# Another order of waits at four places of a two-block transformer kernel

## The chip, the core and the metric

The kernel runs on one core of a Trainium2 chip. A core has five engines with instruction queues of their own, which run in order and wait for each other by semaphores: TensorE (PE: matmuls and transposes, into PSUM), VectorE (DVE), ScalarE (ACT), GpSimd (POOL) and SyncE (SP, which issues the weight DMAs). PSUM has eight banks of 128 x 512 floats. The metric is the time of one execution on the device, in microseconds.

## What is computed

One sequence of 512 tokens of width 1024 goes through two blocks, all in float32. Cut to what matters here:

```
# first block
h = rmsnorm(x); proj = h @ w_in            # fox q,k,v; sb q,k,v; forget logits
x += concat(rmsnorm(fox_attention(...)), rmsnorm(stick_breaking_attention(...))) @ w_out
x += memory_cross_attention(rmsnorm(x), rmsnorm(mem)) @ w_mo
u = causal_dwconv(rmsnorm(x) @ w_up); gate, val = split(u)
x += (silu(gate) * val) @ w_down           # 2816 gated features
h = rmsnorm(x) * gain                      # the first block's output
# second block, layer 0: gated MLP with spatial gating
z = gelu(rmsnorm(h) @ a_w_in); u, v = split(z); v = layernorm(v)
sv = w_s (masked, per 128-token block and group) @ v + b_s
h += (u * sv) @ a_w_out                    # u, v are 2048 wide
h += relu(rmsnorm(h) @ w1)**2 @ w2
# layer 1: latent attention, then the same MLP; a last rmsnorm
```

## The kernel before

**Products.** A float32 product is made of three matmuls: each operand is a high half (rounded to float32r by ScalarE) and a low half (the rest, by VectorE), and `split_sum` (L424) adds hi x hi, lo x hi and hi x lo in one bank (L432 to L434, or L469 to L471 where tokens are stationary). Activations lie feature-major in `x` (eight tiles of 128 x 512); their halves are in `h_hi`/`h_lo` (eight tiles) and `g_hi`/`g_lo` (four).

**Weights** come as a stream of chunks of 1 MB (`weight_stream`, L61), two slots, each loaded by SP into `raw`, split by ScalarE (`split_high`, L1639, two pieces a chunk, line L1649) and then by VectorE (`split_low`, L935, L944). ScalarE waits until PE has used up the chunk two before (a count of finished tiles that the stream gives, `ENDS`); entries `("tiles", n)` of the stream stand for tiles that need no weights. Both engines call the splits at fixed places of their programs, written out by hand.

**Tiles.** PE fills four banks in turn. `next_bank` waits until the tile four before has been taken; `full` counts a finished tile; on VectorE `take` waits for the next full tile and empties it, always in order. So a VectorE queue that is busy with something else holds PE once four banks are full.

**Attention** is a pipeline over 32 units (head, block of 128 queries), one a step: at step s PE makes the scores of unit s, the values of unit s-3 and the transposes of unit s-2, and then runs what `n_after(s)` gives: other products in pieces, to fill the steps. Unit s-2 needs its probabilities: in fox attention from ScalarE, in sb (stick-breaking) attention from ScalarE's two sigmoids and VectorE's scan and product (L1051, L1054). Beside fox run the memory keys and the sb values; the last three steps (32 to 34) have nothing beside them. The sb queries and keys follow (`by_feature`), then sb attention. Beside it (`beside_sb`, PE L687, DVE L1216, ACT L1812) four transposes per tile turn the mixed, normed fox result into features (`turn_mixed`, L634; ScalarE's high half and VectorE's low half, `take_mixed`, L1191, empty them) at steps 0 and 1, memory values run at steps 2 to 25 in pieces of six matmuls, two pieces a step at first (`MEM_VALUES_AT`), and half of the output product at 26 to 33. `SB_PIECES` are the steps at which VectorE splits a piece of weights (ScalarE one step earlier). After each eight units VectorE copies the bank of results (L1169) and ScalarE sums squares of it.

**The gated feed-forward.** Pairs of 256 gated features (granules) go through `up`, a convolution and a gate, into `t_buf`; their halves go to two of the four `g` tiles. `down` (PE L506, DVE L1013, ACT L1695) multiplies two granules: its first half of four output tiles, then four more, each added to `x`. The eleventh granule (number 10) is left over and goes through `back(10)` (PE L486) after the last `down`. Its halves are made at the end of that `down` (`then=`), since the four `g` tiles are still being read. `back("final, mix0")` on VectorE and ScalarE also makes the next halves in `h` and the squares for two statistics (`two_stats`, L769; VectorE's sums L983).

**The gated MLP of block two.** Four groups of values `gm_v`, then sixteen feature tiles of `gm_u` (taken at L1030, gelu at L1890). After tile 13 PE makes group 0 of the spatial products (`spatial`, L794, four tiles), tiles 14 and 15, and `out_half(0, 0)`, which reads the halves of the gated product in `g`. On VectorE: `take_spatial` (L1396, with biases made just before, L1391), `times_u` (L1404), `low_of_gated` (L1409); on ScalarE `high_of_gated`.

## Time and profile before

| | us |
|---|---|
| three runs | 2068.95, 2066.1, 2068.57 |
| median | 2068.57 |
| the profiled execution | 2069.1 |
| its span in the trace | 2065.8 |
| PE busy in it | 2014.6 (98%) |
| DVE / ACT / POOL busy | 1155.7 / 757.4 / 203.9 |
| mean granted clock of PE | 0.993 |

A busy share says how long an engine had work in it, not how fast it ran: PE's clock has two levels, 2.4 and 1.2 GHz, and PEclk is the share of full speed that was granted. A timeline row gives the start, the duration, the engine, the source line, what is written from what, how many instructions were merged, and in brackets the idle time ahead of it with what ended it. Matmul durations overlap: one of 128 x 512 has 0.39 us, but the next starts 0.23 us later.

### The profile page before, as it was taken

To read this page: it belongs to the slowest core of one execution; us is meant where nothing else is said; L and a number is where in the kernel's file an instruction comes from. 1 tells how busy PE (TensorE), PEld (TensorE's weight loads), DVE (VectorE), ACT (ScalarE), POOL (GpSimd) and SP (SyncE) were. 2 spreads that over 40 slices of the span, in tenths; PEclk is the share of its full clock that TensorE was granted. 3 is DMA by queue.
4 is the path that set the end of the run, shared out by engine and by line. 5 is a ranking of instruction groups with operands and counts; after the bars stand their busy time and mean duration, and the time that the engine had idled before them with its cause. 6 is when DMAs were issued, how large, how long until landed. Compare 5 with 4: busy or idle time off the path is not lost. (4 is left out here: it accounts for less than half of the span.)

```text
span 2065.8 us, 23160 instructions
## 1 busy us (share of the span) xinstructions
PE 2014.6 (98%) x9535; PEld 1668.3 (81%) x9535; DVE 1155.7 (56%) x1585; ACT 757.4 (37%) x1201; POOL 203.9 (10%) x108
## 2 busy tenths in 40 slices
PE   7999999999999999999999999999999999999998
PEld 5897888788888888788878888888877788888887
DVE  6543576568756666846557643543487665333333
ACT  4354354235433333533223422233343443322224
POOL 1000000000000000000000222222221002122221
PEclk9999999999999999999999999999999999999999
DMA  5231212212233233233312233223223012232321
GB/s 167 83 99 45 82 62 72 92 42 86 98 102 100 85 102 102 82 106 98 102 62 82 88 102 102 85 99 102 82 66 102 21 62 84 100 102 91 95 101 61
DMA packets 141224, 180.51 MB, mean 87 GB/s; under 512 B 9664, under 2 KB 102976, under 8 KB 141120
## 3 DMA queue, kind: packets, MB, share of 16 engines
q1 hardware_dynamic: 139232, 177.52, 26.5%
q8 instruction: 75, 1.23, 0.2%
q10 hardware_dynamic: 1632, 1.51, 0.2%
q14 instruction: 29, 0.24, 0.0%
q0 software_dynamic: 256, 0.02, 0.0%
HBM read 176.91 MB, written 2.10 MB: 87 GB/s over the span
## 5 line engine op out<-in xcount | busy, mean ns | idle before, releaser
L432 PE MATMUL bank<-h_hi,w_hi 128*128 128x512 f32 x1376 | 542.4, 394 | 7.1 <-DVE arena L1556 4.5
L433 PE MATMUL bank<-h_lo,w_hi 128*128 128x512 f32 x1376 | 537.3, 391 | 0.0
L434 PE MATMUL bank<-h_hi,w_lo 128*128 128x512 f32 x1376 | 537.3, 390 | 0.0
L1649 ACT ACTIVATE w_hi<-raw 128x1024 fp32r<-128x1024 f32 (+2 forms) x336 | 332.7, 1033 | 512.4 <-PE bank L434 456.3
L432 PE MATMUL bank<-g_hi,w_hi 128*128 128x512 f32 (+1 forms) x988 | 384.1, 389 | 9.6 <-DVE g_lo L958 4.3
L434 PE MATMUL bank<-g_hi,w_lo 128*128 128x512 f32 (+1 forms) x988 | 378.8, 383 | 0.0
L433 PE MATMUL bank<-g_lo,w_hi 128*128 128x512 f32 (+1 forms) x988 | 378.7, 383 | 0.0
L402 POOL TENSOR_TENSOR w_lo<-raw,w_hi 128x1024 fp32r<-128x1024 f32 (+1 forms) x78 | 189.5, 2430 | 1658.9 <-ACT w_hi L1649 1658.9
L1002 DVE TENSOR_TENSOR resid<-bank,resid 128x512 f32<-128x512 f32 x288 | 195.9, 689 | 263.2 <-PE bank L434 262.8
L944 DVE TENSOR_TENSOR w_lo<-raw,w_hi 128x1024 fp32r<-128x1024 f32 (+1 forms) x258 | 304.8, 1206 | 67.7 <-ACT w_hi L1649 66.8
L432 PEld LDWEIGHTS bank<-h_hi,w_hi 128*128 128x128 f32 x1376 | 259.4, 189 | 64.5 <-issue 11.0
L433 PEld LDWEIGHTS bank<-h_lo,w_hi 128*128 128x128 f32 x1376 | 259.6, 189 | 55.2 <-issue 1.9
L434 PEld LDWEIGHTS bank<-h_hi,w_lo 128*128 128x128 f32 x1376 | 259.4, 189 | 54.1
L432 PEld LDWEIGHTS bank<-g_hi,w_hi 128*128 128x128 f32 x988 | 186.4, 189 | 48.9 <-issue 12.6
L434 PEld LDWEIGHTS bank<-g_hi,w_lo 128*128 128x128 f32 x988 | 186.2, 188 | 36.5
L433 PEld LDWEIGHTS bank<-g_lo,w_hi 128*128 128x128 f32 x988 | 186.4, 189 | 34.8
L596 PE MATMUL bank<-arena 128*128 128x128 f32 (+8 forms) x928 | 178.6, 328 | 3.3 <-ACT arena L1728 1.4
L596 PEld LDWEIGHTS bank<-arena 128*128 128x128 f32 (+1 forms) x928 | 133.3, 191 | 28.3 <-issue 9.6
L1496 DVE SCALAR_TENSOR_TENSOR arena<-bank,rstd 128x512 f32<-128x512 f32 x64 | 44.0, 691 | 177.4 <-PE bank L434 177.2
L1937 ACT ACTIVATE arena<-arena 128x512 f32<-128x512 f32 x64 | 40.5, 633 | 221.6 <-DVE arena L1496 221.6
L1728 ACT ACTIVATE arena<-bank 128x128 f32<-128x128 f32 (+3 forms) x112 | 48.2, 431 | 174.1 <-PE bank L588 174.1
L958 DVE TENSOR_TENSOR g_lo<-arena,g_hi 128x512 fp32r<-128x512 f32 x110 | 73.7, 688 | 30.7 <-ACT g_hi L1938 20.6
(199 smaller groups left out, 1686.8 us busy)
## 6 DMA issues: line engine op xcount, KB each, us to landing
raw<-w SPq DMA_DIRECT2D x64, 1024.0 KB, 5.2
raw<-w_up SPq DMA_DIRECT2D x22, 1024.0 KB, 5.1
raw<-a_w_in SPq DMA_DIRECT2D x16, 1024.0 KB, 5.2
raw<-w_in SPq DMA_DIRECT2D x12, 1024.0 KB, 5.4
raw<-w_down SPq DMA_DIRECT2D x11, 1024.0 KB, 4.9
raw<-w_mkv SPq DMA_DIRECT2D x8, 1024.0 KB, 5.5
raw<-a_w_out SPq DMA_DIRECT2D x8, 1024.0 KB, 5.0
raw<-w_out SPq DMA_DIRECT2D x4, 1024.0 KB, 5.0
```

The costliest lines, as they stand in the source:

```text
L402: G.tensor_tensor(lo, src, hi.bitcast(F32), ALU.subtract).then_inc(w_split_pool, 1)
L432: nc.tensor.matmul(dst, a_hi, b_hi, start=(k == 0), stop=False)
L433: nc.tensor.matmul(dst, a_hi, b_lo, start=False, stop=False)
L434: last = nc.tensor.matmul(dst, a_lo, b_hi, start=False, stop=(k == n - 1))
L596: ins = nc.tensor.matmul(dst, a, b, start=first, stop=last)
L944: V.tensor_tensor(lo, src, hi.bitcast(F32), ALU.subtract).then_inc(w_split, 1)
L958: V.tensor_tensor(lo, src, hi.bitcast(F32), ALU.subtract).then_inc(ready, 1)
L1002: take(lambda b: V.tensor_tensor(x[:, n, :], b[:], x[:, n, :], ALU.add))
L1496: take(lambda b: V.scalar_tensor_tensor(r_buf[:, j, :], b[:], 0.0, rstd[:, 0, :], ALU.max, ALU.mult))
L1649: A(hi, src, ACT.Copy).then_inc(w_hi_done, 1)
L1728: A(prob_t[:, u % 2, 0:nk], pt_bank[:, 0:nk], ACT.Copy).then_inc(pt_taken, 1)
L1937: A(t_buf[:, j, :], r_buf[:, j, :], ACT.Square)
```

## The change

Four places change; the arithmetic and the number of instructions stay.

1. **Gated MLP.** VectorE takes the four spatial tiles before it splits the chunk that it split after tile 13, and makes the gated low halves before it takes tiles 14 and 15. ScalarE makes the high halves before the gelus of tiles 14 and 15.
2. **Last granule.** The halves of granule 10 go to tiles 6 and 7 of `h`, which nothing reads then, and are made before the last `down`, not at its end. `back(3, in_h=True)` reads them (3 is the pair of h tiles). Because the next halves overwrite tiles 6 and 7, ScalarE waits in every such `back` for PE's eighth tile before it writes tile 6.
3. **Beside sb.** Memory values run at steps 0 to 23 (two pieces a step up to 7), the mixed fox tiles are turned at steps 4 and 8 and taken one step later by VectorE. The stream's counts and `SB_PIECES` follow.
4. **The tail of fox attention.** At steps 32, 33 and 34 PE runs the first tile of the sb queries in parts of three, three and two of its eight triples, not after the tail.

The core of the diff, by engine: the stream and the tables, PE, VectorE (`gated_low` on), ScalarE (from `if n == 6` on):

```diff
-    out += [("tiles", 4)] + mkv(4, 5, 6, 7) + down("w_out", 0) + [("tiles", 4)] + down("w_out", 1)
+    out += mkv(4) + [("tiles", 2)] + mkv(5) + [("tiles", 2)] + mkv(6, 7) + down("w_out", 0) + [("tiles", 4)] + down("w_out", 1)
...
-        MEM_VALUES_AT = [s for s in range(2, 10) for _ in range(2)] + list(range(10, 26))
+        MEM_VALUES_AT = [s for s in range(8) for _ in range(2)] + list(range(8, 24))
+        TURN_AT = (4, 8)
...
-        FOX_PIECES, SB_PIECES = (5, 6, 9, 10, 13, 14, 18, 20, 27, 28, 33, 34), (1, 2, 7, 8, 11, 12, 19, 21, 27, 29)
+        FOX_PIECES, SB_PIECES = (5, 6, 9, 10, 13, 14, 18, 20, 27, 28, 33, 34), (1, 2, 5, 6, 10, 12, 18, 20, 27, 29)
...
+            def first_queries(ks):
+
+                if ks[0] == 0:
+                    wait_chunk()
+                dst = next_bank() if ks[0] == 0 else tile_bank[tile.n % 4]
+                last = split_sum(dst[:], w_tiles(KT, slice(0, P)), h_tiles(), part=ks)
+                if ks[-1] == KT - 1:
+                    full(last)
+
             def beside_fox(s):
+                if s >= len(BLOCKS):
+                    n = 3 * (s - len(BLOCKS))
+                    first_queries(range(n, min(n + 3, KT)))
...
-            for c in range(4):
+            by_feature(first=1)
+            for c in range(3):
                 by_feature()
...
             def beside_sb(s):
-                if s < 2:
-                    if s == 0:
-                        pe.wait_ge(t_made, 2)
-                    turn_mixed(2 * s)
-                    turn_mixed(2 * s + 1)
+                if s in TURN_AT:
+                    pe.wait_ge(t_made, 2)
+                    turn_mixed(2 * TURN_AT.index(s))
+                    turn_mixed(2 * TURN_AT.index(s) + 1)
...
-            back(10)
+            back(3, in_h=True)
...
             def gated_low(pair):
                 dve.wait_ge(t_made, made.n)
                 for j in range(2):
-                    lo_g(pair, j, t_buf[:, j, :])
+                    if pair < 10:
+                        lo_g(pair, j, t_buf[:, j, :])
+                    else:
+                        low_half(h_lo[:, 6 + j, :], h_hi[:, 6 + j, :], t_buf[:, j, :], None, h_ready)
...
-                down(then=lambda: gated_low(2 * n + 2))
+                if n < 4:
+                    down(then=lambda: gated_low(2 * n + 2))
+            gated_low(10)
+            down()
...
-                if n % 2:
+                if n % 2 and n < 13:
                     split_low()
...
             take_spatial(0)
+            split_low()
...
+            for j in range(4):
+                low_of_gated(0, j)
             for n in (14, 15):
                 take(scaled(gm_u[:, n, :], rstd[:, 1, :]))
-            for j in range(4):
-                low_of_gated(0, j)
...
                 for n in range(KT):
                     taken()
+                    if n == 6:
+                        act.wait_ge(tile_full, tile.n + 1)
                     prep(n, name)
...
-            down(then=lambda: hi_g(10))
+            for j in range(2):
+                made.n += 1
+                act.wait_ge(t_made, made.n)
+                high_half(h_hi[:, 6 + j, :], t_buf[:, j, :])
+            down()
...
+            high_of_gated(0)
             for n in (14, 15):
...
-            high_of_gated(0)
```

Lines of the changed kernel are up to 27 higher. VectorE in the gated MLP, before: from the take of tile 13 (the first row) to the first additions of the output product. The fourth row is the spatial takes, the seventh the gated low halves.

```order
L1030 TENSOR_TENSOR arena<-bank,rstd 128x512
L944 TENSOR_TENSOR w_lo<-raw,w_hi 128x1024 x2
L1391 SCALAR_TENSOR_TENSOR biases<-arena,vec 128x128 x4
L1400 SCALAR_TENSOR_TENSOR arena<-bank,vec,biases 128x512 x4
L1406 TENSOR_TENSOR arena<-arena 128x512 x4
L1030 TENSOR_TENSOR arena<-bank,rstd 128x512 x2
L958 TENSOR_TENSOR g_lo<-arena,g_hi 128x512 x4
L944 TENSOR_TENSOR w_lo<-raw,w_hi 128x1024 x2
L1391 SCALAR_TENSOR_TENSOR biases<-arena,vec 128x128 x4
```

The same stretch now:

```order
L1043 TENSOR_TENSOR arena<-bank,rstd 128x512
L1410 SCALAR_TENSOR_TENSOR biases<-arena,vec 128x128 x4
L1419 SCALAR_TENSOR_TENSOR arena<-bank,vec,biases 128x512 x4
L957 TENSOR_TENSOR w_lo<-raw,w_hi 128x1024 x2
L1425 TENSOR_TENSOR arena<-arena 128x512 x4
L971 TENSOR_TENSOR g_lo<-arena,g_hi 128x512 x4
L1043 TENSOR_TENSOR arena<-bank,rstd 128x512 x2
L957 TENSOR_TENSOR w_lo<-raw,w_hi 128x1024 x2
L1410 SCALAR_TENSOR_TENSOR biases<-arena,vec 128x128 x4
```

The split went behind the spatial takes, the low halves ahead of the two takes of tiles 14 and 15.

VectorE around the last down projection of block one, before: the gate product, eight adds to `x` with a split between them, the low halves of granule 10.

```order
L1298 TENSOR_TENSOR arena<-arena 128x512 x2
L1002 TENSOR_TENSOR resid<-bank,resid 128x512 x4
L944 TENSOR_TENSOR w_lo<-raw,w_hi 128x1024 x2
L1002 TENSOR_TENSOR resid<-bank,resid 128x512 x4
L958 TENSOR_TENSOR g_lo<-arena,g_hi 128x512 x2
L944 TENSOR_TENSOR w_lo<-raw,w_hi 128x1024 x2
```

Now:

```order
L1311 TENSOR_TENSOR arena<-arena 128x512 x2
L971 TENSOR_TENSOR h_lo<-arena,h_hi 128x512 x2
L1015 TENSOR_TENSOR resid<-bank,resid 128x512 x4
L957 TENSOR_TENSOR w_lo<-raw,w_hi 128x1024 x2
L1015 TENSOR_TENSOR resid<-bank,resid 128x512 x4
L957 TENSOR_TENSOR w_lo<-raw,w_hi 128x1024 x2
```

The two low halves stand ahead of the first adds, and are written to `h_lo`.

PE at the start of sb attention, before: scores (bank 4 or 5, with the mask), two turned tiles a step (from `mixed`, in the arena), and the first probabilities' transpose into bank 6 at step 2.

```order
L596 MATMUL bank4<-arena 128x128
L596 MATMUL bank4<-masks 128x128
L638 MATMUL bank1<-ident,arena 128x128 x4
L638 MATMUL bank2<-ident,arena 128x128 x4
L596 MATMUL bank5<-arena 128x128
L596 MATMUL bank5<-masks 128x128
L638 MATMUL bank3<-ident,arena 128x128 x4
L638 MATMUL bank0<-ident,arena 128x128 x4
L596 MATMUL bank4<-arena 128x128
L596 MATMUL bank4<-masks 128x128
L588 MATMUL bank6<-ident,arena 128x128
L432 MATMUL bank1<-w_hi,g_hi 128x256
```

Now, with repeated matmuls left out:

```order
L597 MATMUL bank4<-arena 128x128
L597 MATMUL bank4<-masks 128x128
L433 MATMUL bank1<-w_hi,g_hi 128x256
...
L597 MATMUL bank5<-arena 128x128
L597 MATMUL bank5<-masks 128x128
L433 MATMUL bank1<-w_hi,g_hi 128x256
...
L597 MATMUL bank4<-arena 128x128
L597 MATMUL bank4<-masks 128x128
L589 MATMUL bank6<-ident,arena 128x128
L433 MATMUL bank1<-w_hi,g_hi 128x256
```

Steps 0 and 1 run memory values (`g_hi` holds the halves of the memory) where the turned tiles stood, and the transpose into bank 6 follows these.

## Rows read from the trace of the kernel before

**Rows 1.** The page, part 1: busy time and share of the span.
```profile
PE 2014.6 (98%) x9535; PEld 1668.3 (81%) x9535; DVE 1155.7 (56%) x1585; ACT 757.4 (37%) x1201; POOL 203.9 (10%) x108
```

**Rows 2.** PE timeline: start us, us, engine, line, operation, count, [idle before, releaser].
```profile
190.91 1.11 PE L596 MATMUL bank<-arena 128*128 128x64 f32 x8 [0.69 <-ACT arena L1728]
...
242.84 0.44 PE L588 MATMUL bank<-ident,arena 128*128 128x128 f32 x1 [2.32 <-DVE arena L1054]
...
269.58 0.44 PE L588 MATMUL bank<-ident,arena 128*128 128x128 f32 x2 [1.05 <-DVE arena L1054]
...
290.99 0.55 PE L588 MATMUL bank<-ident,arena 128*128 128x128 f32 x3 [0.50 <-DVE arena L1054]
...
840.85 0.47 PE L432 MATMUL bank<-g_hi,w_hi 128*128 128x512 f32 x1 [2.17 <-issue]
...
865.79 1.12 PE L536 MATMUL bank<-arena,ones 128*128 128x512 f32 x2 [1.25 <-DVE arena L983]
...
1029.98 0.47 PE L432 MATMUL bank<-h_hi,w_hi 128*128 128x512 f32 x1 [1.96 <-DVE arena L1400]
...
1046.82 0.77 PE L432 MATMUL bank<-g_hi,w_hi 128*128 128x512 f32 x1 [4.08 <-DVE g_lo L958]
```

**Rows 3.** Windows: width, busy PE, PEld, DVE, ACT, POOL; PEclk, DMA share, GB/s.
```profile
242.80:246.50 3.70, 3.66 (x19) 3.66 (x20) 3.53 (x7) 1.12 (x4) 0.00 (x0) 0.54 0.06 16
340.80:344.00 3.20, 3.20 (x14) 2.67 (x15) 3.20 (x5) 2.66 (x4) 0.00 (x0) 1.00 0.00 0
841.00:850.00 9.00, 9.00 (x40) 7.43 (x41) 8.88 (x13) 6.75 (x11) 0.00 (x0) 1.00 0.66 217
1031.50:1035.00 3.50, 3.50 (x10) 2.75 (x9) 2.71 (x5) 0.00 (x0) 0.00 (x0) 0.53 0.27 105
1046.80:1052.00 5.20, 5.18 (x13) 4.10 (x14) 5.00 (x9) 0.64 (x2) 0.00 (x0) 0.51 0.09 9
1063.70:1067.00 3.30, 3.30 (x18) 2.74 (x17) 2.37 (x5) 1.23 (x2) 0.00 (x0) 1.00 0.00 0
```

**Rows 4.** DVE timeline, gated MLP.
```profile
1025.63 2.36 DVE L944 TENSOR_TENSOR w_lo<-raw,w_hi 128x1024 fp32r<-128x1024 f32 x2 [0.46 <-ACT w_hi L1649]
...
1029.08 2.73 DVE L1400 SCALAR_TENSOR_TENSOR arena<-bank,vec,biases 128x512 f32<-128x512 f32 x4
...
1031.72 2.49 DVE L1406 TENSOR_TENSOR arena<-arena 128x512 f32<-128x512 f32 x4
...
1045.98 2.50 DVE L958 TENSOR_TENSOR g_lo<-arena,g_hi 128x512 fp32r<-128x512 f32 x4 [2.51 <-ACT g_hi L1664]
```

**Rows 5.** ACT timeline, gated MLP.
```profile
1045.27 2.17 ACT L1664 ACTIVATE g_hi<-arena 128x512 fp32r<-128x512 f32 x4
```

**Rows 6.** ACT timeline, start of sb attention.
```profile
239.81 1.06 ACT L1649 ACTIVATE w_hi<-raw 128x1024 fp32r<-128x1024 f32 x1
```

**Rows 7.** DVE timeline, sb attention, step 18.
```profile
279.85 0.69 DVE L1169 COPY arena<-bank 128x512 f32<-128x512 f32 x1 [1.22 <-PE bank L596]
...
280.45 0.87 DVE L1096 TENSOR_SCALAR arena<-bank,rstd_col 128x256 f32<-128x256 f32 x2
```

**Rows 8.** DVE timeline, tile adds after memory attention and last down projection.
```profile
484.67 0.74 DVE L960 SCALAR_TENSOR_TENSOR h_lo<-resid,vec,h_hi 128x512 fp32r<-128x512 f32 x1
...
485.93 0.74 DVE L960 SCALAR_TENSOR_TENSOR h_lo<-resid,vec,h_hi 128x512 fp32r<-128x512 f32 x1
...
826.72 2.48 DVE L1002 TENSOR_TENSOR resid<-bank,resid 128x512 f32<-128x512 f32 x4
...
839.45 1.29 DVE L958 TENSOR_TENSOR g_lo<-arena,g_hi 128x512 fp32r<-128x512 f32 x2
...
857.28 8.45 DVE L983 TENSOR_TENSOR arena<-arena 128x2048 f32<-128x2048 f32 x6
```

**Rows 9.** ACT timeline, last down projection.
```profile
838.72 0.63 ACT L1664 ACTIVATE g_hi<-arena 128x512 fp32r<-128x512 f32 x1 [9.11 <-PE bank L434]
```

**Rows 10.** PE timeline, turn of the mixed sb result.
```profile
338.51 1.91 PE L638 MATMUL bank<-ident,arena 128*128 128x128 f32 x16
```

More of the change, by code:

```diff
@@ L446, in w_tiles, with by_feature @@
                 return [(view(w_hi, slot)[:, k, cut], view(w_lo, slot)[:, k, cut]) for k in range(n)]
-            def by_feature(tiles=2, moving=None, arrive=None, n_tokens=S):
+            def by_feature(tiles=2, moving=None, arrive=None, n_tokens=S, first=0):
                 wait_chunk()
-                for j in range(tiles):
+                for j in range(first, tiles):
                     dst = next_bank()[:, 0:n_tokens]
@@ L710, in of_fox @@
                     chunk.n += 1
-            fox_end = tile.n + 4
+            fox_end = tile.n + 8
             attention("sb", BLOCKS, sb_scores, head_values(sb_v), beside_sb, late=lambda s: max(0, 3 - s // 2))
@@ L1216, in beside_sb @@
             def beside_sb(s):
-                if 1 <= s < 3:
-                    take_mixed(h_hi, h_lo, "fox_out_g", 2 * s - 2)
-                    take_mixed(h_hi, h_lo, "fox_out_g", 2 * s - 1)
+                if s - 1 in TURN_AT:
+                    for j in range(2):
+                        take_mixed(h_hi, h_lo, "fox_out_g", 2 * TURN_AT.index(s - 1) + j)
                 for c in range(4):
@@ L1812, in beside_sb @@
             def beside_sb(s):
-                if s < 2:
-                    high_of_mixed(h_hi, "fox_out_g", 2 * s)
-                    high_of_mixed(h_hi, "fox_out_g", 2 * s + 1)
+                if s in TURN_AT:
+                    tile.n += 1
+                    for j in range(2):
+                        high_of_mixed(h_hi, "fox_out_g", 2 * TURN_AT.index(s) + j)
                 squares_of_group(4, SB_PIECES)(s)
@@ L1820, in _ @@
             made.n += 1
-            tile.n += 4 + 4
+            tile.n += 2 + 4
             split_high()
@@ L1868, in _ @@
                     down(then=lambda: hi_g(2 * n + 2))
-            down(then=lambda: hi_g(10))
+            for j in range(2):
+                made.n += 1
+                act.wait_ge(t_made, made.n)
+                high_half(h_hi[:, 6 + j, :], t_buf[:, j, :])
+            down()
             act.dma_start(ws_stage, w["a_w_s_2"].rearrange("g i j -> i g j")).then_inc(gm_loaded, 16)
```

## The prediction

> **What bounds the kernel now.** I read the page first: TensorE (PE) is busy for 2014.6 of 2065.8 us [rows 1], so whatever an order of waits can win lies in the 51 us in which PE stands, and in what its clock loses around them. Next came PE's timeline, where each row carries the idle time ahead of it and who ended it [rows 2]. Then the windows, where PEclk is the granted clock as a share of 2.4 GHz [rows 3]; time lost to it is width x (1 - PEclk). The edits touch four places, in order of time:
>
> A, the tail of fox attention: waits of 0.69 us for ScalarE's copy of a transposed tile [rows 2]; there are two of them, 1.38 us.
> B, sb attention: one wait of 2.32 us at its start, behind which the clock is 0.54 for 3.7 us (1.7 us lost), and four small ones of 0.50 to 1.05, all for VectorE's product at L1054 [rows 2, 3].
> C, the last down projection of the first block: 2.17 us ahead of the last granule, and 1.25 us at the second of two statistics, which waits for VectorE's sum of squares [rows 2]. No clock is lost at the first [rows 3].
> D, the gated MLP: 1.96 us for the first spatial tile's bank, 4.08 us for the gated halves, and behind them a clock of 0.53 for 3.5 us and 0.51 for 5.2 us, so 1.6 + 2.5 us [rows 2, 3]. Together 10.1 us in 25: by far the largest.
>
> **D, spatial tiles and gated halves first.** VectorE now finishes the take of u tile 13, splits a weight chunk (2.36 us from 1025.63) and only then takes the spatial tiles; PE, done with them at 1028.0 (1029.98 less 1.96), waits for the first bank [rows 2, 4]. Moved behind the four takes, the split leaves only the biases (from 1027.9 to 1029.1, 1.1 us) ahead of them, so they start at about 1026.3, as the first tile fills, and keep step with PE; the bank is free before 1028.0. Who needs the split? The chunk is that of the first a_w_out quarter, first used after tiles 14 and 15. The chunk of those two tiles was split one step earlier. PE then runs 48 matmuls of 0.229 us (14 in 3.2 us [rows 3]) and reaches the output product at 1039.0. VectorE: last take 1028.9, split to 1031.3, four products (2.49) to 1033.8, lows (2.50) to about 1036.4, behind ScalarE's high halves (2.17), which no longer stand behind the gelu of tile 15 [rows 4, 5]. Slack 2.6 us. Moved behind the lows are the takes of 14 and 15 (banks wanted only from the third output tile) and, on ScalarE, two gelus, wanted when the next spatial products start. Tile 14 is taken at 1037.1 instead of on arrival; PE asks for its bank at 1044. So both waits go, and with them the clock losses: 10.1 us. If the clock fell there anyway, 6.0 us remain. That it need not is seen at the next spatial group, whose matmuls run into the output product with no wait and a clock of 1.00 [rows 3]. What comes late next: the split of the second quarter, held by ScalarE until tile 15 is full, as before; relative to PE it is where it was.
>
> **A, queries between the last values.** 24 matmuls of the first sb query tile, which PE ran right behind the tail, go 9, 9 and 6 between its steps. 9 x 0.229 = 2.1 us covers each wait of 0.69. Their weights were split four steps earlier and their bank was taken. Each return from small matmuls costs the first large one some 0.1 us, twice more. Gain 1.2 us (0 to 1.4). VectorE's norm of fox's result starts 2.6 us later and holds its first query take, but its bank is wanted only four tiles later.
>
> **B, memory values first.** At steps 0 and 1 PE now runs two times 12 matmuls of memory values where eight transposes of the mixed result stood in each, and VectorE no longer takes two mixed tiles (0.7 us each) ahead of the first product. It still has one split piece there (1.2 us, half of 2.36 [rows 4]), which starts when ScalarE's half is done: 1.06 us from 238.6, since the two high halves (1.2 us) ahead of 239.81 are gone [rows 6]. The first product ends at about 241.7; PE, now with 2 x 1.45 us of memory values ahead of it, asks at 241.5. The 2.32 becomes about 0.25, and the 1.7 of clock goes: gain 3.8. Then the price. The two turning steps (4 and 8) load VectorE with 1.4 us of takes beside a split: 0.5 us of waits in all. At steps 10 and 18 VectorE has the copy of o_bank (0.69) and, at step 18 today and in the same way at 10, the memory values (0.87) [rows 7]; the changed table puts a split piece (1.2) beside the copy instead: 0.35 longer each, plus the 0.3 by which it arrives late at step 10. The piece of step 21 (a wait of about 0.5) goes to 20, whose ScalarE half stands behind the squares of a group at step 19: as at step 12 today, that makes about 1.1, 0.6 more. Steps 24 and 25 lose their matmuls (they went to steps 0 and 1), and VectorE takes memory values at 24: about 0.4. Sum of the price 2.5, so B gives 1.3. Ends: 3.8, if none of the new waits shows, and -1, if each is twice what I say.
>
> **C, the last granule in h's idle tiles.** High and low halves of granule 10 no longer wait for g's tiles, so they are made ahead of the projection instead of at its end, and the 2.17 us go. But VectorE's lows now stand ahead of the takes which free PE's banks. Today VectorE starts these at 826.72, just in time: PE, done with the first half at 827.3, resumes at once [rows 8]. From ScalarE's high halves to VectorE's last low are 2.0 us (838.72 to 840.74) [rows 8, 9]; they can start at 826.2, after the first product, so the takes start at 828.3, 1.55 us late, and PE waits 1.55 us at 827.5. The granule starts at 840.2, 0.6 earlier. ScalarE's weight split at that point hangs on the end of the projection, now 840.2: VectorE starts the granule's takes 0.6 later than today. It catches up at 1.26 us a tile (484.67 to 485.93) against PE's 6 x 0.229 = 1.37, and ends about 0.15 late; from there the split and the sums of squares (8.45 us) run to the second statistic, where PE waits today and will wait longer [rows 8]. So the gain is handed back: +0.2 us (ends -0.9, if the lows hide, and +1.5, if the longer wait costs clock as at D). The added wait on ScalarE (seventh tile behind PE's eighth, in all three such places) ends before ScalarE gets there, as it trails PE; behind it stands only the next tile, wanted 4 us later: nothing.
>
> **The sum.** -10.1 - 1.2 - 1.3 + 0.2 = -12.4 us. The profiled execution took 2069.1 us (span 2065.8), the runs' median is 2068.57; from the median, 2056.2.
>
> **A rule against it.** At 338.5 sixteen transposes and a wait of 0.35 are followed by large matmuls at a clock of 1.00 [rows 3, 10]. The Trainium skill, "TensorE: Matmul & The Clock Gate", section "Part 4: PE-mode transpose", says that transposes do not count as busy time for the clock gate in the way matmuls do. By that rule the turning steps 4 and 8, transposes between small matmuls and short waits, could drop the clock; by the row they don't. Worked out below as a rival, from rows.
>
> **The rivals.**
> 1. The clock at D stays low by itself. For it: the fall at 1031.5 comes 1.5 us after PE resumed, not at once, and waits of 2.17 us elsewhere cost nothing. Against: the second spatial group at 1.00 [rows 3]. D gives 6.0 only, the sum is -8.3: 2060.3. Chance 0.10.
> 2. C's lows hide and B's new waits don't show: -10.1 - 1.2 - 3.8 - 0.9 = -16.0: 2052.6. Chance 0.10.
> 3. The turning steps cost clock, twice the 1.7 us of today's start [rows 3]: -9.0: 2059.6. Chance 0.07.
> 4. D's new order isn't in time, the lows come 3 us later than I say (a weight half late on ScalarE): a wait of 0.5 to 3 us and its clock are back: -12.4 + 5 : 2061.2. Chance 0.04.
> 5. Slower than before: sb attention from step 8 on becomes bound by VectorE, PE idles at each step, and the clock falls to half for the stretch. From 256 to 300 us that is 44 us at 0.5, up to 22 us lost; 2068.6 - 12.4 + 22 = 2078. It turns the sum from 12.4 us lost on, that is 25 us at half clock. Against: waits of 0.50 to 1.05 stand there now without a fall. Chance 0.02.
> 6. The change does not do what it says at A and B (a wait on a chunk's split in their place): -9.9: 2058.7. Chance 0.05.
> The forecast, within 2.5 us, has the rest, 0.62.
>
> **The numbers.** 2056.2; 2052 to 2061 leaves out rival 5, and halves of 2 and 4: under 0.2 with the forecast's own tails. A measurement of this kernel can tell about 0.2% (4.1 us) from no change: faster means below 2064.4, which only rival 5 and an unforeseen loss miss: faster 0.94, same 0.04, slower 0.02.
>
> **What would show it.** D: PE's rows hold no wait between the spatial matmuls and the output product, PEclk is 1.00 from 1020 on. A: no waits at L1728. B: no 2 us wait at sb's start, and waits of about 1.1 at steps 11, 13, 19 and 21. C: a new wait of 1.5 us ahead of the second half of the last projection, none ahead of the granule, and 2 us instead of 1.25 at the second statistic. Wrong it would be, if D's low halves end after PE reaches the output product, or if the clock still falls there.

## The result, and the profile after

The changed kernel takes **2055.47 us** (median of 4 runs, 2054.94 to 2058.22), the kernel before 2067.70 beside it (4 runs, 2066.10 to 2068.95): a ratio of **0.9946 [0.9932, 0.9959]**. The forecast was 2056.2, with 2052 to 2061 around it. The profiled execution is the slowest of the four, 2058.22 us with a span of 2056.0.

The busy times on the page answer to [rows 1]: the same 9535 matmuls, and TensorE (PE) idle for 43.0 us of the span instead of 51.2.

```profile
PE 2013.0 (98%) x9535; PEld 1667.0 (81%) x9535; DVE 1155.7 (56%) x1585; ACT 757.6 (37%) x1201; POOL 203.7 (10%) x108
```

Now PE's timeline of the changed kernel, with the columns of [rows 2]: at the four places every row with 0.5 us or more of idle time ahead of it, and three rows of the latent attention behind them. L433, L537 and L589 are the L432, L536 and L588 of before; VectorE's L1054, L983 and L1002 have become L1067, L996 and L1015.

```profile
260.92 0.44 PE L589 MATMUL bank<-ident,arena 128*128 128x128 f32 x2 [0.74 <-DVE arena L1067]
266.25 0.44 PE L589 MATMUL bank<-ident,arena 128*128 128x128 f32 x2 [1.38 <-DVE arena L1067]
279.85 0.33 PE L589 MATMUL bank<-ident,arena 128*128 128x128 f32 x1 [0.96 <-DVE arena L1067]
286.01 0.55 PE L589 MATMUL bank<-ident,arena 128*128 128x128 f32 x3 [1.11 <-DVE arena L1067]
825.42 0.47 PE L433 MATMUL bank<-g_hi,w_hi 128*128 128x512 f32 x1 [1.52 <-DVE resid L1015]
862.23 2.08 PE L537 MATMUL bank<-arena,ones 128*128 128x512 f32 x2 [2.27 <-DVE arena L996]
1504.50 0.50 PE L433 MATMUL bank<-g_hi,w_hi 128*128 128x512 f32 x1 [1.14 <-DVE w_lo L957]
1531.88 0.47 PE L433 MATMUL bank<-h_hi,w_hi 128*128 128x512 f32 x1 [1.84 <-DVE arena L1576]
1557.59 0.55 PE L433 MATMUL bank<-h_hi,w_hi 128*128 128x512 f32 x1 [2.67 <-DVE arena L1576]
```

The two waits of the gated MLP, the one at sb's start, the two of the fox tail and the one ahead of granule 10 are gone. Four stand beside sb, one is new at 825, and the one at the second statistic is 1.0 longer. The last three rows are of places that the change doesn't touch; the same waits stand in the kernel before.

Windows of the changed kernel, cut to PE (width, busy PE with matmuls, granted clock, DMA share, GB/s): fox tail and sb queries, sb's start, its middle, the 10 us behind the wait at the second statistic, the gated MLP, and the 10 us behind the last of the waits above.

```profile
190.00:237.00 47.00, 47.00 (x225) 1.00 0.29 90
237.00:256.00 19.00, 19.00 (x164) 1.00 0.35 113
256.00:300.00 44.00, 39.62 (x281) 1.00 0.15 48
862.23:872.23 10.00, 10.00 (x26) 0.52 0.01 2
1020.00:1060.00 40.00, 40.00 (x210) 1.00 0.17 61
1557.59:1567.59 10.00, 10.00 (x37) 0.83 0.61 210
```

The kernel before behind its own waits at the same statistic and in the latent attention (1568.83), and in the gated MLP:

```profile
865.79:875.79 10.00, 10.00 (x39) 0.83 0.01 2
1020.00:1060.00 40.00, 33.96 (x148) 0.87 0.20 69
1568.83:1578.83 10.00, 10.00 (x44) 1.00 0.62 210
```

In the gated MLP PE stood for 6.04 us of 40 at a mean clock of 0.87 and now stands for none at 1.00. Against that, the 10 us behind the last wait, which nobody changed, ran at 1.00 before and run at 0.83 now: 1.7 us lost. Behind the second statistic 4.8 us are lost, where the kernel before lost 1.7.

Start-to-start distances between PE rows of both traces give the sum part by part. They count the waits and the clock alike:

| stretch | before | after | difference | forecast |
|---|---|---|---|---|
| first fox scores to first sb scores (A) | 137.61 | 135.77 | -1.84 | -1.2 |
| first sb scores to the turn of sb's result (B) | 100.79 | 98.45 | -2.34 | -1.3 |
| the turn to the first of two statistics, and to the second (C) | 527.28 | 527.39 | +0.11 | +0.2 |
| second statistic to the next statistic, 80 us later | 80.56 | 83.48 | +2.92 | 0 |
| spatial group to the next one (D) | 35.91 | 25.35 | -10.56 | -10.1 |
| two statistics of the latent attention and behind it (1550.20 to 1714.47; 1538.96 to 1704.76) | 164.27 | 165.80 | +1.53 | 0 |

The four parts come to -14.6 us. The trace gives back 2.9 and 1.5 by a clock at half, behind the second statistic and at 1558. The other three executions of the changed kernel have a span of 2052.8 to 2053.6 at a mean clock of 0.995 or 0.996, against 0.993 here. So what is given back differs from one execution to the next, and the experiments had to say where.

### The profile page after: what moved, and what is told of

It reads as the page before. It is cut to its first block and busy times, and to the rows that moved or that the text cites. A ratio compares the mean times of both kernels' runs of the same rounds, so it can differ in the third digit from the quotient of the medians.

```text
span 2056.0 us, 23165 instructions
## 1 busy us (share of the span) xinstructions
PE 2013.0 (98%) x9535; PEld 1667.0 (81%) x9535; DVE 1155.7 (56%) x1585; ACT 757.6 (37%) x1201; POOL 203.7 (10%) x108
## 3 DMA queue, kind: packets, MB, share of 16 engines
q8 instruction: 76, 1.25, 0.2%
q10 hardware_dynamic: 1632, 1.51, 0.2%
## 5 line engine op out<-in xcount | busy, mean ns | idle before, releaser
L433 PE MATMUL bank<-h_hi,w_hi 128*128 128x512 f32 x1392 | 549.0, 394 | 4.7 <-DVE arena L1576 4.5
L434 PE MATMUL bank<-h_lo,w_hi 128*128 128x512 f32 x1392 | 544.0, 391 | 0.0
L435 PE MATMUL bank<-h_hi,w_lo 128*128 128x512 f32 x1392 | 543.9, 391 | 0.0
L433 PE MATMUL bank<-g_hi,w_hi 128*128 128x512 f32 (+1 forms) x972 | 376.7, 388 | 4.9 <-DVE resid L1015 1.5
L435 PE MATMUL bank<-g_hi,w_lo 128*128 128x512 f32 (+1 forms) x972 | 371.7, 382 | 0.0
L434 PE MATMUL bank<-g_lo,w_hi 128*128 128x512 f32 (+1 forms) x972 | 371.5, 382 | 0.0
L1015 DVE TENSOR_TENSOR resid<-bank,resid 128x512 f32<-128x512 f32 x288 | 195.7, 688 | 260.6 <-PE bank L435 260.3
L433 PEld LDWEIGHTS bank<-h_hi,w_hi 128*128 128x128 f32 x1392 | 262.7, 189 | 62.7 <-issue 8.8
L433 PEld LDWEIGHTS bank<-g_hi,w_hi 128*128 128x128 f32 x972 | 182.7, 188 | 42.5 <-issue 7.1
```

Of the source, the lines that this page charges most:

```text
L433: nc.tensor.matmul(dst, a_hi, b_hi, start=(k == 0), stop=False)
L434: nc.tensor.matmul(dst, a_hi, b_lo, start=False, stop=False)
L435: last = nc.tensor.matmul(dst, a_lo, b_hi, start=False, stop=(k == n - 1))
L1015: take(lambda b: V.tensor_tensor(x[:, n, :], b[:], x[:, n, :], ALU.add))
```

## The experiments

Ratios are to the kernel before, run beside each group of kernels: 2067.69 us (20 runs) beside the first four, 2067.49 (13) beside the next four, 2068.12 (19) beside the last four.

### Each part alone

The first four ask whether each stretch's gain is the gain of its own part, and whether it reaches the total. The gated MLP's edits on top of the kernel before:

```diff
-                if n % 2:
+                if n % 2 and n < 13:
                     split_low()
...
             take_spatial(0)
+            split_low()
...
+            for j in range(4):
+                low_of_gated(0, j)
             for n in (14, 15):
                 take(scaled(gm_u[:, n, :], rstd[:, 1, :]))
-            for j in range(4):
-                low_of_gated(0, j)
...
+            high_of_gated(0)
             for n in (14, 15):
...
-            high_of_gated(0)
```

> The kernel before with the new order of the gated MLP alone (spatial tiles and gated halves first). If the two waits (1.96 and 4.08 us) and the low clock behind them go together, the time falls by 10.1 us, ratio 0.9951, and PEclk is 1.00 from the spatial matmuls into the output product. If the clock falls there whatever the waits, 6.0 us (0.9971) and windows at 0.5 remain. If this part is not most of the gain, less than 6 us.

Measured: 2060.67 us (5 runs, 2056.21 to 2062.21), 0.9963 [0.995, 0.9976]: 7.0 us, an interval from 5.0 to 10.3 that holds both the 10.1 and the 6.0 of the expectation, though the stretch is 25.35 us long as in the changed kernel, 10.56 less. PE's rows at the two unchanged waits of 1533 and 1560, and windows behind them, of this kernel:

```profile
1533.03 0.47 PE L432 MATMUL bank<-h_hi,w_hi 128*128 128x512 f32 x1 [1.85 <-DVE arena L1557]
1560.39 0.47 PE L432 MATMUL bank<-h_hi,w_hi 128*128 128x512 f32 x1 [2.67 <-DVE arena L1557]
```

```profile
1533.90:1537.20 3.30, 3.30 (x10) 0.50 0.00 0
1561.00:1564.60 3.60, 3.60 (x11) 0.53 0.70 274
1572.00:1582.00 10.00, 10.00 (x46) 1.00 0.28 98
```

Both waits, here as long as in the kernel before, are followed by a spell at half clock, 3.3 us in all; before has neither. First reading: D wins 10.56 and 3.3 are handed back later.

The last granule alone (high and low halves in h's idle tiles, ahead of the projection) on top of the kernel before:

```diff
-            back(10)
+            back(3, in_h=True)
...
-                down(then=lambda: gated_low(2 * n + 2))
+                if n < 4:
+                    down(then=lambda: gated_low(2 * n + 2))
+            gated_low(10)
+            down()
```

> The kernel before with the last granule in h's tiles alone. My account: the wait of 2.17 us goes, one of 1.5 us comes ahead of the second half of the projection, and the second statistic waits 2.3 us in place of 1.25; with the clock as it was 0.2 us slower (1.0001), with the longer spell at half clock that the changed kernel's trace shows up to 3 us slower (1.0015). The rival, that the part gives its 2.17 us: 0.9990.

Measured: 2067.78 us (10 runs), 1.0002 [0.9992, 1.0011]. PE's waits of this kernel in the stretch:

```profile
829.07 0.47 PE L432 MATMUL bank<-g_hi,w_hi 128*128 128x512 f32 x1 [1.52 <-DVE resid L1002]
...
865.88 1.12 PE L536 MATMUL bank<-arena,ones 128*128 128x512 f32 x2 [2.27 <-DVE arena L983]
```

The 2.17 is gone, 1.52 has come ahead of the second half and 1.02 at the statistic: +0.1 us by starts, as in the changed kernel. C only moves a wait.

sb's part alone (memory values at the first steps, the two turns at steps 4 and 8, the changed table of pieces; the diff stands above):

> The kernel before with memory values first beside sb alone. My account: the start of sb has no wait of 2.3 us and no low clock (3.8 us), four waits of 0.7 to 1.4 us take the place of four of 0.5 to 1.05: from the first sb scores to the turned sb tiles 98.5 us in place of 100.8, ratio 0.9989. The rival, that this part gives nothing and the tail of fox gives it: 100.8 us and 1.0000.

Measured: 2065.00 us (10 runs), 0.9987 [0.9978, 0.9997]: 2.7 us, and 98.43 us for sb's stretch (-2.36), with fox's stretch as before (137.60). This trace holds something else. Its two waits at the gated MLP are 1.96 and 4.08 us as before, but windows behind them read:

```profile
1031.50:1035.00 3.50, 3.50 (x17) 1.00 0.13 50
1045.60:1048.70 3.10, 3.10 (x9) 0.50 0.03 8
```

The clock fell behind the second wait only, and the MLP's stretch is 33.53 us instead of 35.91. So the 1.6 us of [rows 3] at 1031.5 are lost in some executions and not in others.

The changed kernel without C:

> The changed kernel with the last granule put back in g's tiles. If that part costs 0.2 to 3 us, this is 0.2 to 3 us faster than the changed kernel (ratio to before 0.9930 to 0.9945, the changed kernel's is 0.9946); if it gains 2 us, this has 0.9956.

Measured: 2057.19 us (4 runs), 0.9949 [0.9934, 0.9964], not to be told from the changed kernel's 0.9946. The wait of 2.17 is back, this time with a spell behind it that the kernel before does not have at 841 [rows 3]:

```profile
835.70:839.20 3.50, 3.47 (x9) 0.53 0.83 278
```

### Half of D, and three attempts to get more

The changed kernel with the gated halves back behind u tiles 14 and 15 on both engines, the spatial tiles still first:

> The changed kernel with the gated halves back behind the takes and gelus of tiles 14 and 15; the spatial tiles still come first. If the halves were late because of their place in the two queues, PE waits 4 us again ahead of the output product, with low clock behind it or not; from one spatial group to the next 29.5 us without the clock and 32 with it, in place of 25.35, and the time is 4 to 7 us above the changed kernel (0.9965 to 0.998). If the spatial order alone is enough, 25.35 us and 0.9946.

Measured: 2063.09 us (10 runs), 0.9975 [0.9965, 0.9984], 0.003 or 6 us more than the changed kernel's ratio. The 4.08 us are back at full length (PE row at 1042.06) with their half clock, and the stretch is 31.29 us, 5.94 more. With the split's move alone the 1.96 us are gone and the 4.08 stand, so the halves' move is what wins these. No kernel here has the halves' move alone.

The second statistic one token tile later, so that VectorE's squares would be covered:

```diff
-            def two_stats():
-                stat(sq[:, 0, :], by_col=True)
-                stat(sq_normed[:, 0, :], by_col=True, bank=s_bank[0], col_at=TT)
-
-            by_token(arrive=h_n.n, between=two_stats)
+            by_token(arrive=h_n.n, between=lambda: stat(sq[:, 0, :], by_col=True),
+                     after_first=lambda: stat(sq_normed[:, 0, :], by_col=True, bank=s_bank[0], col_at=TT))
```

> The changed kernel with the second of the two statistics behind the first token tile of the second half. If PE only stands there because VectorE's sums come late, its wait of 2.3 us goes and so does the low clock behind it: 2.3 to 5 us less than the changed kernel (0.9925 to 0.9935). If the wait moves to the takes that need both statistics, nothing is won (0.9946).

Measured: 2056.40 us (4 runs), 0.9943 [0.9928, 0.9958]: nothing. The statistic no longer waits, but the next token tiles do. PE's row, and VectorE's timeline of this kernel (start us, us, engine, line, operation, count, [idle before, releaser]):

```profile
873.93 0.80 PE L470 MATMUL bank<-w_hi,h_hi 128*128 128x512 f32 x1 [2.58 <-DVE w_lo L956]
```

```profile
852.31 8.46 DVE L995 TENSOR_TENSOR arena<-arena 128x2048 f32<-128x2048 f32 x6
860.69 3.34 DVE L1006 RECIPROCAL rstd<-rstd 128x512 f32<-128x512 f32 x1
...
866.64 3.35 DVE L1006 RECIPROCAL rstd<-rstd 128x512 f32<-128x512 f32 x1 [0.98 <-ACT rstd_col L1701]
...
871.53 2.35 DVE L956 TENSOR_TENSOR w_lo<-raw,w_hi 128x1024 fp32r<-128x1024 f32 x2
```

VectorE has only 1 us of idle time from the squares at 852.31 to the split at 871.53, which PE waits for. The second reciprocal starts later because the statistic does, and the split stands behind it. VectorE is the bound of this place; moving what PE does there only chooses where it waits.

sb's split pieces at other steps, off those at which VectorE copies o_bank, and ScalarE's squares ahead of them where they stood in the way:

```diff
-        FOX_PIECES, SB_PIECES = (...), (1, 2, 5, 6, 10, 12, 18, 20, 27, 29)
+        FOX_PIECES, SB_PIECES = (...), (1, 2, 6, 7, 12, 14, 20, 22, 27, 29)
...
-                squares_of_group(4, SB_PIECES)(s)
+                squares_of_group(4, (1, 2, 5, 6, 10, 11, 17, 18, 27, 29))(s)
```

> The changed kernel with other steps for the weight pieces beside sb: VectorE at (1, 2, 6, 7, 12, 14, 20, 22, 27, 29), ScalarE's halves one or more steps earlier than now. If the waits at steps 11, 13, 19 and 21 come from a piece beside the copy or behind ScalarE's squares, they fall from 4.35 us in all to under 1.5: from the first sb scores to the turned sb tiles 95 to 96 us in place of 98.4 (ratio 0.993 to 0.9935). If VectorE is simply full there, 98 us and 0.9946.

Measured: 2052.07 us (4 runs), 0.9924 [0.9909, 0.9938]; sb's stretch is 93.37 us, 5.08 less than in the changed kernel. PE's waits beside sb fall to one of 0.16 us. A window of its middle:

```profile
256.00:300.00 44.00, 43.80 (x306) 1.00 0.14 48
```

39.62 us of matmuls have become 43.80. So all four waits came from where the pieces stood, as the prediction's price list of B says, and they could be had back whole. This kernel moves VectorE's pieces and ScalarE's together; which of the two ended which wait it doesn't tell. The runs' interval touches that of the changed kernel; the 5 us stand on the trace.

The lows of granule 10 behind the first four takes instead of ahead of them:

```diff
                     if n == 3:
+                        middle()
                         split_low()
...
-            gated_low(10)
-            down()
+            down(middle=lambda: gated_low(10))
```

> The changed kernel with the low halves of the last granule behind VectorE's first four takes of the last projection. If these lows hold PE there, the wait of 1.5 us goes with no new one, but the second statistic still waits for the sums: some 0.6 to 1 us less than the changed kernel (0.9941 to 0.9943). If the wait is ScalarE's, it stays and nothing changes.

Measured: 2055.28 us (4 runs), 0.994 [0.9925, 0.9955]. The wait of 1.52 is gone and no other has come; from the turn to the first of the two statistics are 521.80 us, 1.51 less, and the second waits 2.27 as before. The runs' times alone can't show 1.5 us; the trace does.

### Where D's gain went

This pair leaves out two reciprocals of a 128x512 row in the second latent attention, 3.35 us each on VectorE, which stand ahead of the waits of 1.85 and 2.67 us; a multiplication by 1 takes their place.

```diff
-                ins = V.reciprocal(row, row)
+                ins = V.tensor_scalar(row, row, 1.0, None, ALU.mult) if leave else V.reciprocal(row, row)
...
-            finish_rstd(rstd[:, 1, :])
+            finish_rstd(rstd[:, 1, :], leave=True)
...
-                    finish_rstd(rstd_kv, rstd_col[:, 8:12])
+                    finish_rstd(rstd_kv, rstd_col[:, 8:12], leave=True)
```

> The kernel before, with the two reciprocals of a 128x512 row in the second latent attention (3.35 us each on VectorE) left out: a multiplication by 1 stands in their place, so these two norms are not inverted and the output is not the reference's. It is the base for the next run. The two waits of PE behind these reciprocals (1.85 us near 1540 us of the span, 2.67 near 1568) lose up to 2.7 us of their cause each. Expected: both waits gone, 4.0 to 4.5 us less, ratio 0.998, and no half clock between 1530 and 1580, as in the kernel before itself.

> The same two reciprocals left out, and part D (spatial tiles and gated halves first) on top: the difference to f1_short_recip is D's worth where the two waits behind it no longer stand. D alone gave 7.0 us in time (5 runs) while its own stretch was 10.56 shorter. Theory 'handed back at the next waits' (the clock fell behind the waits of 1.85 and 2.67 us in that execution, which cost 3 us): without these waits nothing can fall there, so 10.0 to 10.6 us less than f1_short_recip, ratio about 0.993 against the kernel before. Rival 'D's stretch overstates': the loss lies elsewhere or in the level of all executions, and the difference stays near 7 us, ratio 0.9945.

Measured: f1 2063.95 us (10 runs), 0.9978 [0.9968, 0.9987]; f2, with D, 2054.60 us (4 runs), 0.9937 [0.9922, 0.9951]. By the medians D is worth **9.35 us** where the two waits don't stand. With four runs of f2 (2053.24 to 2059.51) that is uncertain by 3 us or so, which reaches down to e1's 7.0: the times alone leave open whether D gives more here. The traces say more. Windows of f1, then of f2:

```profile
1020.00:1060.00 40.00, 33.96 (x166) 0.96 0.21 73
1530.00:1580.00 50.00, 48.62 (x204) 1.00 0.36 108
1046.20:1048.90 2.70, 2.70 (x8) 0.50 0.03 9
```

```profile
1020.00:1060.00 40.00, 40.00 (x211) 1.00 0.18 61
1530.00:1580.00 50.00, 48.56 (x211) 1.00 0.32 106
```

Between 1530 and 1580 both now run at 1.00, with one wait of 1.38 us at 1569 (1560 in f2) left. From the statistic behind the MLP to the one behind the latent attention f1 takes 1156.11 to 1709.20 and f2 1146.70 to 1699.79, both 553.09 us; the kernel before takes 556.46 there, the changed one 557.95, e1 559.63. So in this pair of traces nothing of D's gain is lost behind it, and what is lost in the others stands behind those two waits. And f1 had only one of the two spells at the MLP, as e3: in this pair of traces D won 8.1 us at its place, and the other 1.3 of 9.4 between the spans (2060.5 and 2051.1) come from a spell in f1's start-up, from 14.9 to 21.7 us, that f2 does not have.

The fox tail alone: the first sb query tile's 24 matmuls between the last values, on the kernel before.

> The kernel before with part A alone: the first sb query tile's 24 matmuls between the last fox values. Theory by starts: first fox scores to first sb scores 135.8 us instead of 137.6, both waits for ScalarE's copy gone; then sb attention starts with its wait as before. 1.8 us less, 2065.8, ratio 0.9991. By the prediction's term it would be 1.2 less. Rival: the norm of fox's result, now later on VectorE, gives a wait at the first query tiles or lengthens the wait of 2.32 us at sb's start, and nothing is left: 2067.6.

Measured: 2065.69 us (10 runs), 0.9989 [0.998, 0.9999]: 2.4 us, with fox's stretch 135.77 us (-1.84). This kernel has neither D nor B nor C, and yet, behind its wait of 2.67 us at 1564.59, the clock falls:

```profile
1565.70:1569.20 3.50, 3.50 (x11) 0.53 0.69 275
```

So the first reading of e1 does not stand as it is: the spell there doesn't need D, and the kernel before can have been spared it in the one execution that was profiled. That D makes it likelier is not excluded. Behind this wait a spell stands in all eight traces that contain D or half of it, and in one of the four without; behind the wait of 1.85 us in three of the eight and none of the four.

Last, the changed kernel with the edits of e7 and e8 together:

> The changed kernel with the two edits that won: the split pieces beside sb at other steps (5.1 us less in its stretch) and the lows of the last granule behind the first four takes (1.5 us less). They lie 450 us apart, so they should add: 2055.5 - 5.1 - 1.5 = 2048.9. If the clock falls behind one more of the remaining waits, as it did in several of these kernels, 2050.5. Ratio 0.991 to 0.992.

Measured: **2051.19 us** (4 runs, 2045.20 to 2051.95), 0.991 [0.9895, 0.9924]: faster than both kernels. By starts the parts add (sb 93.35 us, turn to first statistic 521.83). PE's waits over 1.5 us between 180 and 1600 us of this kernel; there are no others:

```profile
854.07 2.07 PE L537 MATMUL bank<-arena,ones 128*128 128x512 f32 x2 [2.27 <-DVE arena L996]
1523.56 0.47 PE L433 MATMUL bank<-h_hi,w_hi 128*128 128x512 f32 x1 [1.85 <-DVE arena L1576]
1549.27 0.68 PE L433 MATMUL bank<-h_hi,w_hi 128*128 128x512 f32 x1 [2.67 <-DVE arena L1576]
```

The time is 2.3 us above the sum of the stretches (2048.9) and within what the clock does: three of its runs took 2051.1 to 2051.95 us at a mean clock of 0.993 to 0.995, the fourth 2045.20 at 0.998.

## Why the prediction was right, and where it was not

The total came out within 0.8 us, by parts that were each in the right place and of the right sign. Alone they gave 2.4 (A), 2.7 (B), -0.1 (C) and 7.0 us (D), 12.0 in all; together 12.2. The runs show no sign that they disturb each other, within the 2 to 3 us that they can tell. That the total is off by 0.8 us and not by more is partly luck. By starts A and B gave 1.7 us more than their terms, D's term took more than it gives in the mean of the traces, and the added losses behind the second statistic and at 1558, 4.5 us in the profiled execution, are in no term.

**D, right.** VectorE's timeline of the changed kernel, which answers to [rows 4]:

```profile
1024.45 1.13 DVE L1410 SCALAR_TENSOR_TENSOR biases<-arena,vec 128x128 f32<-128x128 f32 x4
1025.61 2.73 DVE L1419 SCALAR_TENSOR_TENSOR arena<-bank,vec,biases 128x512 f32<-128x512 f32 x4
1028.25 2.35 DVE L957 TENSOR_TENSOR w_lo<-raw,w_hi 128x1024 fp32r<-128x1024 f32 x2
1030.52 2.49 DVE L1425 TENSOR_TENSOR arena<-arena 128x512 f32<-128x512 f32 x4
1032.93 2.49 DVE L971 TENSOR_TENSOR g_lo<-arena,g_hi 128x512 fp32r<-128x512 f32 x4
1035.34 0.68 DVE L1043 TENSOR_TENSOR arena<-bank,rstd 128x512 f32<-128x512 f32 x1
```

Biases, takes, split, products, lows, then u tile 14: the order and, to 0.1 us each, the durations of the prediction. The takes to the lows lie 0.6 to 1.0 us earlier than it says, since this place itself comes 0.6 earlier. The lows end at 1035.4; PE's first matmul of the output product starts at 1038.10. The slack is 2.7 us where 2.6 was worked out. That rules out rival 4, and PEclk 1.00 over 1020 to 1060 rules out rival 1: the clock at D fell because of D's waits.

What was wrong in this term is how sure it was. It took both spells of the one profiled execution as lost every time. Of the five traces in which both waits stand, two lost 1.7 us behind the first and 2.5 behind the second, three nothing and 1.7 (windows of 10 us). So the stretch is 35.9 us twice and 33.5 three times. The mean of the five is 34.5, and D is worth 9.1 on that mean; f1 and f2 give 9.35. e1's interval of 5.0 to 10.3 us holds this. So the mechanism was right, and the term of 10.1 was about 1 us too large.

**A, right but sized at 1.2 for 1.84.** The error lies in what a wait costs. The idle time in brackets begins at the modelled end of a matmul, and that lies behind the point at which the next could have started: a row of a 128x512 matmul lasts 0.39 us but the next starts 0.23 after it. Fox's last three groups of values start at 188.78, 190.91 and 193.15 in before and at 189.29, 192.65 and 196.01 after. Less the 9 query matmuls in each gap (9 x 0.228), the gaps fall from 2.13 and 2.24 to 1.31 each. So the two gaps give 1.75 us, with the cost of the returns already taken off, where the prediction had 1.38 less 0.2. The 0.1 us that each return to large matmuls was to cost is real: the first starts 0.31 us ahead of the second and not 0.23, at 194.06 in before, and at 190.49, 193.84 and 196.82 now. At D the same slip makes 6.04 into 6.4.

**B, right by its mechanism, sized at 1.3 for 2.34.** The wait at the start went whole (0.25 had been left to it), with its clock: 19 of 19 us busy at 1.00 from 237. Of the price, the waits of 0.74, 1.38, 0.96 and 1.11 stand at steps 11, 13, 19 and 21, as the prediction says. The 0.5 us at the turning steps and the 0.4 at step 24 aren't there; one wait of 0.16 us stands at step 10. Small waits were 2.9 us before (0.76, 1.05, 0.61, 0.50) and are 4.35 now: a price of 1.4, not 2.5. This price is the term that was mis-sized. e7 shows the cause: with the pieces at other steps all four vanish.

**C, right.** The new wait ahead of the second half is 1.52 us (1.55 was said), none stands ahead of the granule, the statistic waits 2.27 (2 was said), net +0.1 (+0.2). What it missed is the clock. It looked at the clock behind the wait of 2.17 only, and behind the second statistic the kernel before had already lost 1.7 us. In the 10 us behind this statistic the changed kernel's trace lost 4.8 us and e2's 1.7, with the same wait of 2.27 ahead. The end of C's range, +1.5, was to hold that; it holds half.

**The rivals.** 2 needed C's lows hidden and B without new waits: the waits of both are in the trace. 3, clock lost at the turning steps, fell: PEclk is 1.00 over 237 to 256 and 256 to 300, with the turns in the first of these. So in this trace transposes between small matmuls and waits of up to 1.4 us did not lower the clock, as the row at 338.5 had it, and the other seven traces with B lost nothing between 237 and 300 us either. 5 fell with it, and 6 with the two stretches of A and B.

## What to carry to other kernels

Look for the waits in which an engine that has enough time overall is merely in the wrong order; here two such waits and the clock behind them made 9.1 of 12 us by the traces (7.0 by the runs of D alone), and the new order could be worked out to 0.1 us from the durations of one engine's rows. The clock could not: take what it loses behind a wait from several traces before you give it a price. Where the engine is full from its last idle time to the one that PE waits for (C, e6), another order only moves the wait. Take gains of a few us from distances between starts of the same rows in both traces, which showed 0.1 us here where the medians of 4 to 10 runs showed 2 to 3; and before you blame a change for a clock that fell behind an untouched wait, look whether a kernel without the change shows it too.

## What the runs showed of the hardware

The clock falls behind the same wait in one execution and not in the next. Over the 14 traces of this study (each kernel once), with the loss taken from the granted clock of the 10 us from the row behind the wait on, 10 x (1 - PEclk):

| PE's wait, by its idle time | traces with it | followed by half clock | us lost then |
|---|---|---|---|
| 4.08 us, gated halves (1045) | 6 | 6 | 1.7 or 2.5 |
| 2.67 us, latent attention (1560) | 12 | 9 | 1.6 to 1.7 |
| 2.32 us, start of sb (242) | 6 | 5 | 1.7 |
| 2.27 us, second statistic (860), with C | 6 | 6 | 1.7 to 4.8 |
| 2.17 us, granule 10 (840) | 7 | 2 | 1.7 |
| 1.96 us, spatial bank (1030) | 5 | 2 | 1.7 |
| 1.85 us, latent attention (1533) | 12 | 3 | 1.7 |
| 1.52 us, last down projection (825), with C | 5 | 0 | |
| 1.25 us, second statistic (860), without C | 7 | 7 | 1.7 or 3.4 |

A fall costs 1.7 us or about twice or three times that. The length of the wait does not sort the cases: 1.25 us at the statistic was always followed by a spell, 2.17 seldom. The losses of 3.4 and more behind the statistic stand in all seven traces that contain B and this wait, and in none of the six without B, though the rows around the statistic are the same. Whether B gives 1.7 us back there, e3's 2.7 us in the runs against 2.36 in its stretch does not show.

What does sort the cases, after the fact, is where the wait begins. All beginnings and ends of the slow spells of one trace, as the granted clock gives them, lie on one even grid in time, and two executions differ in how their work lies on it. The wait of 1.85 us begins 0.4 to 0.7 us behind a point of the grid in the three traces that have a spell behind it, and 1.3 us or more in the nine that don't. The wait of 1.25 us begins at most 0.4 us from a point in the five traces that lost 1.7 us, and 1.2 and 1.4 us behind one in the two that lost 3.4 (e3 and e4, with B). At no wait of the table do the places with and without a loss mix. On this reading B and D act on these losses only by moving the later work in time. No run here moved the work for that purpose, so it stays a reading of 14 traces and is not shown by an experiment.

In 8 of the 14 a spell (1.7 to 2.5 us lost in the window 17 to 23) also stands in the start-up, within 14.6 to 21.8 us, which no kernel here changes. Together these fit the 2 to 6 us by which executions of one kernel differ, at mean clocks from 0.993 to 0.998. The Trainium skill, "TensorE: Matmul & The Clock Gate", section "Part 1: The HAM clock gate", says that the number of slow matmuls at the start varies from run to run of one kernel, with the phase of the clock gate when the kernel starts. The start-up here agrees, with its spell in 8 traces of 14. What share of the executions of one kernel loses how much behind each wait stays open: it would take many traces of one kernel.
